# One of four weight sums of a sum unit made by an adding DMA from GpSimd, and the order of VectorE and ScalarE around it

## What is computed

```python
D_MODEL, SEQ, D_FF = 2048, 256, 5632

def swiglu(hn, w_in, w_out):
    u = hn @ w_in                      # w_in is 2048 x 11264
    return (jax.nn.silu(u[..., :D_FF]) * u[..., D_FF:]) @ w_out

h = h + swiglu(rmsnorm(h, norm_ffn[layer]), ffn_w_in[layer], ffn_w_out[layer])   # layer 0 and 1
```

## Time and profile before

| | us |
|---|---|
| median of 3 runs | 2030.3 (2030.12 to 2030.91) |
| the profiled execution's own time | 2029.66 |
| its span, first to last instruction | 2027.9 |
| TensorE busy | 1993.6 (98%) |
| VectorE busy | 1440.6 (71%) |
| ScalarE busy | 1054.6 (52%) |
| GpSimd busy | 89.8 (4%) |
| DMA queue of SyncE's loads | 376 MB, 53.9% of 16 engines' time |

### The profile page before, as it was taken

The page is one execution under the profiler, slowest core; times in us unless marked ns, Lnnn a source line. Parts: engine busy times, 40 slices in busy tenths (PEclk is TensorE's granted clock), DMA queues, the critical chain, the costliest instruction groups (busy, mean ns, idle before and its releaser), DMA issues. The chain is left out here.

```text
span 2027.9 us, 26273 instructions
## 1 busy us (share of the span) xinstructions
PE 1993.6 (98%) x9991; PEld 1700.5 (84%) x9991; DVE 1440.6 (71%) x1487; ACT 1054.6 (52%) x1190; POOL 89.8 (4%) x113
## 2 busy tenths in 40 slices
PE   7999999999999999999999999999999999999999
PEld 7999988888888887888897888788888888878887
DVE  6868555789988898444466885569888998864443
ACT  5478435555555555343365664455555555543332
POOL 1130200000000000000002320000000000000000
PEclk9999999999999999999999999999999999999999
DMA  7454653555555557555545335355555555575552
GB/s 272 168 190 163 229 190 106 203 193 201 192 201 200 194 206 248 190 201 189 171 145 176 122 124 180 110 187 194 200 202 192 206 189 205 200 253 189 188 200 88
DMA packets 190161, 378.03 MB, mean 186 GB/s; under 512 B 6122, under 2 KB 10484, under 8 KB 189716
## 3 DMA queue, kind: packets, MB, share of 16 engines
q1 hardware_dynamic: 189648, 376.02, 53.9%
q0 software_dynamic: 272, 1.13, 0.2%
q10 hardware_dynamic: 180, 0.05, 0.0%
HBM read 375.08 MB, written 2.10 MB: 186 GB/s over the span
## 5 line engine op out<-in xcount | busy, mean ns | idle before, releaser
L511 ACT ACTIVATE w_hi<-raw 128x2048 fp32r<-128x2048 f32 (+2 forms) x299 | 563.3, 1887 | 513.7 <-PE bank L1524 314.6
L914 DVE TENSOR_TENSOR w_lo<-raw,w_hi 128x2048 fp32r<-128x2048 f32 (+2 forms) x183 | 410.5, 2249 | 321.4 <-ACT w_hi L511 320.9
L1524 PE MATMUL bank<-w_hi,act_hi 128*128 128x512 f32 (+2 forms) x1184 | 455.4, 385 | 5.8 <-DVE act_lo L950 3.8
L1524 PE MATMUL bank<-w_hi,act_lo 128*128 128x512 f32 (+2 forms) x1184 | 451.6, 381 | 0.0
L1524 PE MATMUL bank<-w_lo,act_hi 128*128 128x512 f32 (+2 forms) x1184 | 451.2, 381 | 0.0
L1609 PE MATMUL bank<-w_hi,act_hi 128*128 128x512 f32 x1048 | 410.2, 391 | 3.6 <-DVE act_lo L919 3.6
L1609 PE MATMUL bank<-w_hi,act_lo 128*128 128x512 f32 x1048 | 408.1, 389 | 0.0
L1609 PE MATMUL bank<-raw_lo,act_hi 128*128 128x512 f32 x1048 | 407.7, 389 | 0.0
L914 DVE TENSOR_TENSOR raw_lo<-raw,w_hi 128x2048 fp32r<-128x2048 f32 x116 | 265.6, 2289 | 98.0 <-ACT w_hi L511 95.8
L1524 PEld LDWEIGHTS bank<-w_hi,act_hi 128*128 128x128 f32 x1184 | 222.3, 188 | 48.8 <-DVE act_lo L950 5.0
L1524 PEld LDWEIGHTS bank<-w_hi,act_lo 128*128 128x128 f32 x1184 | 222.3, 188 | 41.6
(11 more groups left out here) (219 smaller groups left out, 2091.3 us busy)
## 6 DMA issues: line engine op xcount, KB each, us to landing
raw<-in_ffn_w_in SPq DMA_DIRECT2D x176, 1024.0 KB, 5.2
raw<-in_ffn_w_out SPq DMA_DIRECT2D x88, 1024.0 KB, 5.0
raw<-in_lru_w_in SPq DMA_DIRECT2D x32, 1024.0 KB, 5.5
raw<-in_lru_w_out SPq DMA_DIRECT2D x16, 1024.0 KB, 5.0
raw<-in_w_o SPq DMA_DIRECT2D x16, 1024.0 KB, 5.1
raw<-in_w_ukv SPq DMA_DIRECT2D x8, 1024.0 KB, 5.3
raw<-in_w_uq SPq DMA_DIRECT2D x8, 768.0 KB, 4.7
raw<-in_w_dkv SPq DMA_DIRECT2D x8, 576.0 KB, 3.7
```

Of the source, the lines that this page charges most:

```text
L511: A.activation(flat_chunk(w_hi, s, size), flat_chunk(raw, s, size), ACT.Copy).then_inc(w_hi_done, 1)
L914: V.tensor_tensor(flat_chunk(to, s, size), flat_chunk(raw, s, size), flat_chunk(w_hi, s, size).bitcast(F32), ALU.subtract).then_inc(w_lo_d ...
L1524: i = T.matmul(outs[t], x_part, wp, start=first and n == 0, stop=last and n == 2)
```

## The change

In the sum units the sum b12+b22, which is now called t3, is made by a DMA: GpSimd waits until the chunk has landed and issues a transfer of tile b22 from HBM once more (128x512 float32, 256 KB), which adds to tile 2 of the slot at its destination (`accum_op`). That is 3 transfers a block, 10 blocks, 2 stages: 60 in all. ScalarE and VectorE now wait for this transfer (`acc_in`) before they touch the slot. VectorE makes three sums in place of four: t2 = b11+t3, t1 = t2-b22, t4 = t2+b21. ScalarE makes the hi part of the whole slot in one operation of 128x2048 in place of three. VectorE's lo part of the slot comes ahead of the lo part of t1 and t2. And `result_out` now comes before the sums of the next block's unit 2, in block 0 the gated product too; ScalarE splits that chunk behind its silu. TensorE multiplies as before, with other names for two tiles.

```diff
+        acc_in = {s: sem(f"acc_in{s}") for s in (0, 2)}
...
+        def acc_no(f, i, u):
+            return i + S_BLOCKS * f if u % 4 == 0 else 2 * i + (2 * S_BLOCKS * f - (u == 2))
...
             def split_sums(m, s, q, n_acc):                      # ScalarE
-                act.wait_ge(raw_in[s], 16 * m + 16)
+                act.wait_ge(acc_in[s], 16 * n_acc)
                 act.wait_ge(chunk_used, 4 * m + s - 3)
-                A.activation(w_hi[s][:, 0:2, :], raw[s][:, 0:2, :], ACT.Copy)
-                A.activation(w_hi[s][:, 3, :], raw[s][:, 3, :], ACT.Copy)
-                act.wait_ge(t_sum, 3 * q + 1)
+                A.activation(flat_chunk(w_hi, s, KC * W), flat_chunk(raw, s, KC * W), ACT.Copy).then_inc(sum_hi, 1)
+                act.wait_ge(t_sum, 3 * q + 2)
                 A.activation(sum_hi_tiles(s)[:, 0:2, :], sum_tiles(t_raw, s)[:, 0:2, :], ACT.Copy).then_inc(sum_hi, 1)
-                act.wait_ge(t_sum, 3 * q + 2)
-                A.activation(w_hi[s][:, 2, :], raw[s][:, 2, :], ACT.Copy).then_inc(sum_hi, 1)
                 act.wait_ge(t_sum, 3 * q + 3)
...
             def sums(m, s, q, n_acc):                            # VectorE
-                dve.wait_ge(raw_in[s], 16 * m + 16)
+                dve.wait_ge(acc_in[s], 16 * n_acc)
                 dve.wait_ge(chunk_used, 4 * m + s - 3)
-                V.tensor_tensor(t13[:, 0, :], raw[s][:, 0, :], raw[s][:, 2, :], ALU.add)
-                V.tensor_tensor(t13[:, 1, :], raw[s][:, 2, :], raw[s][:, 3, :], ALU.add).then_inc(t_sum, 1)
+                V.tensor_tensor(t2, b11, t3, ALU.add).then_inc(t_sum, 1)
                 dve.wait_ge(t_sum, 3 * q + 1)
-                V.tensor_tensor(raw[s][:, 2, :], t13[:, 0, :], raw[s][:, 3, :], ALU.add).then_inc(t_sum, 1)
-                dve.wait_ge(t_sum, 3 * q + 2)
-                V.tensor_tensor(t4, raw[s][:, 2, :], raw[s][:, 1, :], ALU.add).then_inc(t_sum, 1)
+                V.tensor_tensor(t1, t2, b22, ALU.subtract).then_inc(t_sum, 1)
+                V.tensor_tensor(t4, t2, b21, ALU.add).then_inc(t_sum, 1)
...
                     if u == 6:                                   # VectorE, body
                         shared_out(i, shared)
                         following(i, 5)
...
-                            sums(2 * i + (c0 // 4 + 2), 2, unit_no(f, i + 1, 2))
...
                     if u == 7:
                         result_out(i, result)
-                        if not (isinstance(i, int) and i == FB - 1):
-                            following(i, 6)
-                    if u != 5:
+                        following(i, 6)
+                    if u not in (5, 6):
                         following(i, u)
...
+            def sum_loads(f, c0):                                # GpSimd
+                w = a["ffn_w_in"][f].rearrange("(k p) (h n) -> p h k n", p=P, h=2)
+                for i in range(1, FB):
+                    for u in S_UNITS:
+                        s = u % 4
+                        pool.wait_ge(raw_in[s], 16 * (2 * i + (c0 + u) // 4) + 16)
+                        pool.dma_start(raw[s][:, 2, :], w[:, 1, 2 * u + 1, i * W:(i + 1) * W],
+                                       accum_op=ALU.add).then_inc(acc_in[s], 16)
...
                 if d == 0:
+                    sum_loads(0, C_UP0)
...
             rstd(SS_T, RS + 6, 2, D, rstd_done)
+            sum_loads(1, C_UP1)
```

More of the change, by code:

```diff
@@ L644, in up @@
                         k.then_inc(silu_done, 1)
-                    following(0, u)
+                        following(0, 6)
+                    if u != 6:
+                        following(0, u)
                 with act.Fori(0, S_BLOCKS // 2 - 1) as j:
@@ L951, in stationary, with sums @@
                                 act_hi[:, slot:slot + 4, :].bitcast(F32), ALU.subtract).then_inc(st_lo, 1)
-            def sums(m, s, q):
-                dve.wait_ge(raw_in[s], 16 * m + 16)
+            def sums(m, s, q, n_acc):
+                dve.wait_ge(acc_in[s], 16 * n_acc)
                 dve.wait_ge(chunk_used, 4 * m + s - 3)
-                t13, t4 = sum_tiles(t_raw, s)[:, 0:2, :], sum_tiles(t_raw, s)[:, 2, :]
-                V.tensor_tensor(t13[:, 0, :], raw[s][:, 0, :], raw[s][:, 2, :], ALU.add)
-                V.tensor_tensor(t13[:, 1, :], raw[s][:, 2, :], raw[s][:, 3, :], ALU.add).then_inc(t_sum, 1)
+                b11, b21, t3, b22 = (raw[s][:, n, :] for n in range(4))
+                t1, t2, t4 = (sum_tiles(t_raw, s)[:, n, :] for n in range(3))
+                V.tensor_tensor(t2, b11, t3, ALU.add).then_inc(t_sum, 1)
                 dve.wait_ge(t_sum, 3 * q + 1)
-                V.tensor_tensor(raw[s][:, 2, :], t13[:, 0, :], raw[s][:, 3, :], ALU.add).then_inc(t_sum, 1)
-                dve.wait_ge(t_sum, 3 * q + 2)
-                V.tensor_tensor(t4, raw[s][:, 2, :], raw[s][:, 1, :], ALU.add).then_inc(t_sum, 1)
+                V.tensor_tensor(t1, t2, b22, ALU.subtract).then_inc(t_sum, 1)
+                V.tensor_tensor(t4, t2, b21, ALU.add).then_inc(t_sum, 1)
             def split_sums(m, s, q):
                 dve.wait_ge(sum_hi, 2 * q + 1)
-                V.tensor_tensor(sum_tiles(w_lo_t, s)[:, 0:2, :], sum_tiles(t_raw, s)[:, 0:2, :],
-                                sum_hi_tiles(s)[:, 0:2, :].bitcast(F32), ALU.subtract)
-                dve.wait_ge(sum_hi, 2 * q + 2)
                 dve.wait_ge(t_sum, 3 * q + 3)
@@ L1020, in following @@
                     elif is_sum(i, u):
-                        if u != S_UNITS[0]:
-                            sums(m, s, unit_no(f, i, u))
+                        sums(m, s, unit_no(f, i, u), acc_no(f, i, u))
                         split_sums(m, s, unit_no(f, i, u))
@@ L1060, in body @@
                                 stationary(0, act_slot(0), DOWN_G0[d + 1] + 1)
-                            else:
-                                sums(2 * i + (c0 // 4 + 2), 2, unit_no(f, i + 1, 2))
-                            if not (isinstance(i, int) and i == FB - 1):
-                                continue
                         if u == 7:
                             result_out(i, result)
-                            if not (isinstance(i, int) and i == FB - 1):
-                                following(i, 6)
-                        if u != 5:
+                            following(i, 6)
+                        if u not in (5, 6):
                             following(i, u)
@@ L1090, in up @@
                     if u == 6:
-                        sums(c0 // 4 + 2, 2, unit_no(f, 1, 2))
                         continue
@@ L1629, in sum_unit @@
                 own = [tuple(buf[s][:, n, :] for buf in (w_hi, raw_lo)) for n in range(4)]
-                t1, t3, t4 = ((sum_hi_tiles(s)[:, n, :], sum_tiles(w_lo_t, s)[:, n, :]) for n in range(3))
+                t1, t2, t4 = ((sum_hi_tiles(s)[:, n, :], sum_tiles(w_lo_t, s)[:, n, :]) for n in range(3))
                 s1, s2, s3, s4 = ((s_hi[:, j, r, :], s_lo[:, j, r, :]) for r in range(4))
-                b11, b21, t2, b22 = own
+                b11, b21, t3, b22 = own
                 product(result[0], x_tile(2 * u + 1, 0), b21, False, False)
```

8 lines of the change are left out of this document (6 added, 2 removed).

## The result

| | before | after |
|---|---|---|
| median of 6 runs, us | 2030.6 | 2130.95 (2127.55 to 2138.95) |
| the profiled execution's own time, us | 2029.66 | 2130.22 |

The changed kernel takes 1.0499 times as long, with a 95% interval of 1.0483 to 1.0514: 100 us slower.

The account below looks back on a forecast made before the run. TensorE was taken to bound the kernel. Only the wait for the adding transfer counted: (4.3 - 3.85) x 20 = 9 us at unit 6, nothing at units 2 and 4, giving 2039.5 us, range 2029.5 to 2090.

Parts of the forecast that it names:

- TensorE bounds the kernel, VectorE's saving is worth nothing: Up stage: it runs at TensorE's pace, VectorE is never late, so taking work from VectorE gains nothing.
- 39 us of VectorE's work less, about 20 of ScalarE's: Sum units: one sum of four removed, three slot copies made one; busy times fall, nothing gained on the path.
- `result_out` earlier, the silu of block 0, TensorE's and SyncE's part: nothing: Moved work in the up blocks, unchanged matmuls, and SyncE's queue sharing the DMA engines: each put at nothing of its own.
- The limits: Largest A without delay to TensorE: 3.9 us at unit 6, 4.7 at unit 4, 5.25 at unit 2.
- A: In a sum unit, the time from the chunk's landing to the adding transfer's landing; forecast 4.3 us.
- the prediction's own formula: Each microsecond of A over a unit's limit delays TensorE by as much, in 10 blocks and 2 stages, times 20.
- A = 4.3 us: Sum units: 2.5 us plain transfer, 0.86 second read, 0.86 sharing with the next load, plus pick-up; 9 us lost at unit 6.
- The rows that I had set aside: Program start, rows 11 to 13: GpSimd's packets move only when SyncE's load drains; a 1 KB transfer took 5.1 us.
- Behind the load the transfer waits until its packets end, A = 6.9: Rival at units 2 and 6: next load's packets go first, 94 us lost; chance 0.27 in whole or part.
- The rival's 2124: Total in us if the next load's packets win at both units 2 and 6: 4.7 us a block, times 20.
- The range: Whole kernel: 2029.5 us (hidden) to 2090 (behind the load at unit 6 alone); perhaps 0.12 above, 0.03 below.
- Hidden: Rival: the adding transfer lands within 3.85 us everywhere, TensorE's pace is untouched, time 2030.3 us; chance 0.25.

Follow-up runs that it names:

- tile-first kernel: The change, but SyncE loads a sum unit's chunk in three transfers, tile b12 first, and GpSimd's adding transfer waits for that tile alone: 2029.47 against 2029.25 us.
- the new order alone: The change without adding transfers: four sums on VectorE, `result_out` still ahead of the next block's sums; 2030.56 against 2029.65 us for the kernel before.
- the transfer off the chain: The kernel before plus the 60 adding transfers into a spare tile nobody waits for in the up stage: 2031.12 against 2029.25 us.
- unit 6 or unit 2 alone: The new order with the adding transfer in one unit only: unit 6, 2127.64 against 2029.65 us; unit 2, 2069.78 against 2029.56.
- both kernels with held loads: Next loads wait for GpSimd's issue: the change, units 3, 5, 7 held, 2069.94 us; transfer in unit 6 only, unit 7's load held, 2046.66.
- the long hold: The kernel before, TensorE held ahead of unit 6 once a block by three GpSimd memsets: 2100.96 us, ratio 1.0357.
- the short hold: The kernel before, TensorE held ahead of unit 6 once a block by one GpSimd memset: 2054.7 against 2029.25 us.

## Why the prediction was wrong, point by point

- *TensorE bounds the kernel, VectorE's saving is worth nothing.* Right. The tile-first kernel keeps the saving, and its time is that of before.
- *39 us of VectorE's work less, about 20 of ScalarE's.* Measured 36 and 25.
- *`result_out` earlier, the silu of block 0, TensorE's and SyncE's part: nothing.* Right, shown by the new order alone and, for the shared DMA engines, by the transfer off the chain.
- *The limits: A may be 3.9 us at unit 6 (3.85 in the sum), 4.7 at unit 4, 5.25 at unit 2, with 6.05 from the transfer's landing to the last lo part.* Right; that stretch measured 6.2. With the measured means of A (6.33, 4.40, 6.46 at units 2, 4, 6) the prediction's own formula gives (6.33 - 5.25) x 20 = 21.6 and (6.46 - 3.85) x 20 = 52.2 us; the units' excess was 21.4, and 77.4 with 24 us of low clock in it.
- ***A = 4.3 us, "because the adding transfer is issued 0.28 us ahead of the load that it meets": the step that failed.*** It was worth 43 us at unit 6 and 22 at unit 2. The head start of 0.28 us is used up before GpSimd has begun: it picks the landing up after 0.29 us (the sum had 0.05 for this, from no row), so at 628.64 and 628.65 the two issues start together. Then its issue takes 0.86 us, where I had taken the 0.55 of plain issues; the load's takes 0.60. From the start of the issue to the first packet it is 1.57 us for the adding transfer when nothing is ahead of it, and 1.4 for the load: the load is first by 0.16 us. I had taken the start of an issue for the start of its packets. The rows that I had set aside, in which GpSimd's packets come only when a load drains, pointed the right way.
- *Behind the load the transfer waits until its packets end, A = 6.9.* Where no other stall helps, this is what happened: with unit 6 or unit 2 alone a median of 473 and of 477 of the load's 512 packets are ahead of the transfer's first one, and A is 7.0. In the changed kernel it holds in part: in 36 of 40 cases 71 to 492 packets are ahead, A is 6.5 and 6.3 in the mean, and in block 6 both queues move from then on, 64 packets each in a microsecond. The Trainium skill ("DMA: Bandwidth & Descriptors", "Queues, rings and completion order") says that an engine goes round-robin between queues with work, packet by packet; the trace agrees for that microsecond, but not for the time before it, in which the load goes alone, and whether GpSimd's packets were already queued then the trace doesn't tell. Where the load is late, as in unit 4 and in both kernels with held loads, A is 4.4 to 4.5: the 4.3 was right for a case that unit 6 isn't.
- *The rival's 2124 lay near by chance.* Its 94 us were waits alone. With the measured A the waits come to 21.6 + 52.2 = 74; the 20 us that it had too much stood in for the 24 of low clock that it left out.
- *The range.* It had the load's precedence in it at unit 6 alone, 2090. It left out unit 2, which has nearly the same head start, and the clock: no term of the sum and no rival allowed that TensorE's work itself gets slower behind a wait. 24 of the 100 us are that.
- *Hidden.* At unit 6 A was 4.5 us at the least, and 3.85 would have been needed; at unit 4, with 4.4 in the mean, it was hidden but for one block, as the limit is 4.7. The estimate from the Trainium skill ("DMA: Bandwidth & Descriptors", "Anatomy of one DMA — SWDGE (gpsimd) path") for 256 KB and for twice that was 2.6 and 3.2 us, without the pick-up. An adding transfer with no load's packets ahead took 4.0 to 4.2 from issue to landing (medians of unit 4 and of the held kernels), a plain one at unit 4 3.0; the Trainium skill's figure isn't one for adding transfers, and by these runs it doesn't hold for them.

## What to carry to other kernels

When a new transfer is started by a landing, ask first what else the same event starts: here the landing, the release of the next slot and the next load fell within 0.3 us, and who was first decided 81 us in the kernel with unit 6 alone. Price a transfer from the event to its first packet (pick-up, issue, start), since the issue's start says little; and start it from an earlier event (one tile of the chunk) rather than hold others back, which passes the delay on. Where TensorE is the bound, allow for the slower clock that may follow a new wait of 2 us and more, and don't expect anything from work taken off an engine that nobody waits for.

## What the runs showed of the hardware

- An adding transfer of 256 KB from HBM costs GpSimd 0.86 us to issue against 0.54 for a plain one. It moves in 128 packets of 2 KB, 176 ns each in the median, the plain one in 64 of 4 KB, 159 ns each; packets of 2 KB of SyncE's loads take 84 ns.
- It lands 4.0 to 4.2 us after the issue in the median when no load is ahead of it. When one is, it takes 6.4 to 7.9 with unit 6 alone, and 6.2 in the median at units 2 and 6 of the changed kernel.
- GpSimd started its issue 0.29 us after the landing for which it waited, in the mean of each of the three units.
- A load whose packets start first kept GpSimd's packets away well beyond its lead. With a lead of about 0.2 us in block 6 of the changed kernel they started at 3.2 us after the issue in place of 1.57 (123 packets to none, 630.2 to 631.7 us), and then the two queues took turns, 64 to 64; with unit 6 alone, where the load leads by 0.4 us, they started at 4.4 us in the median.
- Waits of TensorE at unit 6 of more than 2 us came with a granted clock of 0.50 for 3.41 us 14 times of 19 in the changed kernel, 17 times of 20 with the transfer in unit 6 alone and 9 of 20 with the long hold; never with the short hold of 0.9 us. With the transfer in unit 2 alone, whose waits are 1.6 us in the mean and 2.9 at most, it came once, behind a wait of 2.18 us. In the changed kernel the waits with it were 2.2 to 3.3 us, those of unit 6 without it 2.3 to 3.2, and of two waits of 2.52 us in the long hold one had it and the other not, so the length alone doesn't decide; what else does stays open.
